# A pair's projection weights replaced while the last projection with the old ones runs, q and k rows in a ring of four at first, first weights in two parts

## The chip, the core and the metric

The kernel runs on one core of one Trainium2 chip. The metric is the device time of one execution in microseconds (us). Five engines work beside each other and meet only at semaphores: TensorE (PE, and PEld for its weight loads), VectorE (DVE), ScalarE (ACT), GpSimd (POOL) and SyncE (SP), which here only issues transfers.

## The reference, cut to what matters

One decoder layer is computed for 1024 prompt tokens and 64 sample tokens (8 sequences of 8) that share the weights.

```python
h = _rms_norm(x, attn_norm_g)
z = h @ w_in                                  # 1024 -> 3*512 (q, k, v) + 2*512 (a, g)
q = _rms_norm(q.reshape(N, T, 8, 64), q_norm_g)
k = _rms_norm(k.reshape(N, T, 8, 64), k_norm_g)
attn, k_state, v_state = attend(q, k, v)      # three dilated windows, combined
u = a * jax.nn.sigmoid(g)
c = _causal_depthwise(u_ext, conv_w, conv_b)  # 31 taps
c = jax.nn.silu(_layer_norm(c, conv_ln_g, conv_ln_b))
x = x + jnp.concatenate([attn, c], -1) @ w_out
h = _rms_norm(x, ffn_norm_g)
x = x + (jax.nn.silu(h @ w_gate) * (h @ w_up)) @ w_down
```

## The kernel before

Every large product is made of three matmuls (`mm3`): the weights and the activations are cut into a high part (fp32r) and a low part (the rest), and high times high, high times low and low times high are summed in PSUM. A piece of weights (128 x 1024, 512 KB) therefore goes three ways: SP loads it into a `raw` buffer, `high(n)` on ScalarE copies the high part, `low(n)` on VectorE (on GpSimd for some) subtracts to get the low part. `w_hi` and `w_lo` count the pieces.

The program is written out by hand, engine by engine, and its order on each engine is the order of the code. The stages:

- **Start.** x arrives in eight slices of 128 features. ScalarE cuts a slice (`xh`) and squares it (`xq`), VectorE subtracts (`xl`) and adds the squares up in `rb`. TensorE runs the first a/gate group over the slices k = 0 to 7, 18 matmuls for each, with the weights of the pieces 0 and 1. Before the last slice it sums the squares with a column of ones.
- **Conv inputs.** The groups g = 3 to 11 of a and gate, 48 matmuls each. From here on VectorE runs the 31 x 4 convolution taps (`tap`, two instructions each, 1024 prompt and 64 sample columns), spread by the tables `TAPS_AG`, `TAPS_Z0`, `TAPS_END0` and `TAPS_STEP` over whatever else it does.
- **First projection.** For the first pair of heads nine q/k/v projections z = 0 to 8 (one token tile each, 24 matmuls: `qkv(z)`). ScalarE squares q and k (`zsq`) and copies them to `zst`, a ring of two; VectorE sums the squares; ScalarE and VectorE make the root and its reciprocal; GpSimd multiplies the rows (`qk_norm`), TensorE turns them (`turn(z)`, issued ahead of `qkv(z + 2)`), GpSimd multiplies k by its gain and SP stores k from the same rows. The copy of z waits for the store of z - 2 (`k_st`).
- **Attention.** 40 steps n, ten for each of the four pairs of heads: step s = n mod 10 is a sample half (s = 0, 5) or one of eight prompt blocks. On TensorE a step is `scores(n + 1)`, the projection of one tile of the next pair (`qkv`, in steps s = 1 to 9; the last pair has pieces of the output projection and of the layer norm there, `fill`), `turn_probs(n)`, `values(n - 1)`, `turn`. On VectorE it is `mask_min(n + 1)` (mask and minimum of the scores), two or three taps, `normalise(n + 1)`, `square_sum` of the new tile. ScalarE takes the exponentials (`exps`) and copies the turned probabilities to `pt`. TensorE's `scores(n + 1)` waits for `mask_min(n)`, `turn_probs(n)` for `normalise(n)`.
- **Weights of the next pair.** A pair's three pieces lie in `wq`, 24 KB a partition, and are replaced when the last projection with the old ones is done: two high parts at the end of step s = 9 and one in step s = 0, the low parts on VectorE behind `mask_min` in the steps s = 0 (two) and s = 1 (one), where the first projection of the new tiles (s = 1) waits for them. The last pair's steps replace them by the first three pieces of the output projection.
- **Sample outputs.** The outputs of a sample half are scaled on VectorE (`scale_sample`, steps s = 2 and 7), turned on TensorE (`turn_sample`) and copied out of bank 6 on VectorE (`sample_outputs`); `values` of the next four blocks writes the same bank and waits for that copy (`d_se`).
- **After attention.** Output projection, second norm, and the feed-forward part in 11 chunks, from about 500 us to the end; neither is touched but for the place of one `low`.

Of the kernel before, what the change touches and what calls it, by code (L numbers as in the profile page):

```python
# [12 lines left out]
P = 128  # L13
# [92 lines left out]

def z_at(p, s):

    return NT * (p + 1) + s - 1 if p < NPAIR - 1 and s >= 1 else None
# [30 lines left out]
TAPS_STEP = {n: 2 if n % NSTEP in (0, 1, 6, 7) else 3 for n in range((NPAIR - 1) * NSTEP)}  # L140
# [3 lines left out]
def hymba_layer(nc, w_stream, xT, kT_c, v_c, cache_k, cache_v, stT, g1, g2, qg, kg, kgcol, cw, cb, lg, lb,  # L144
# [3 lines left out]
    with ExitStack() as ctx:  # L148
# [107 lines left out]
        def zbank(z):  # L256

            return bank(z % 4 if z < NT else 2 + z % 2, 384)
# [17 lines left out]
        raw_in = [sem(f"raw_in{i}") for i in range(3)]  # L276
        w_hi, w_lo = sem("w_hi"), sem("w_lo")
# [9 lines left out]
        k_st, v_st = [sem("k_stored0"), sem("k_stored1")], [sem(f"v_stored{p}") for p in range(NPAIR)]  # L287
        d_sk = [sem(f"sample_k_in{i}") for i in range(4)]
# [98 lines left out]
        def _(sp):  # L387
# [9 lines left out]
            piece(0)  # L397
            for k in range(4):
                sp.dma_start(xr[:, k, :], xT[k]).then_inc(x_in[k], 16)
                if k == 0:  # L400
                    piece(1)
            for k in range(4, KT):
                sp.wait_ge(x_lo, k - 3)
                sp.wait_ge(xsq, k - 3)
                sp.dma_start(xr[:, k % 4, :], xT[k]).then_inc(x_in[k], 16)
            for dst, src in ((ident[:], ident_d), (g2s, g2), (qgs, qg), (kgs[:], kg),
# [5 lines left out]
            for n in range(2, N_B + 3):  # L412
                piece(n)
# [10 lines left out]
            def store(z):  # L424
# [5 lines left out]
                k_src, v_src = zst[r, z % 2, P:2 * P], (vn[p % 2][:, t, :] if t < NT - 1 else vfar[r, 1, p % 2, :])  # L430
# [5 lines left out]
                sp.dma_start(k_dst, k_src).then_inc(k_st[z % 2], 16)  # L436
# [62 lines left out]
            for j in range(2):  # L499
                sp.wait_ge(k_st[j], 16 * NZ // 2)  # L500
# [13 lines left out]
        def _(pool):  # L514
# [25 lines left out]
            def qk_norm(z):  # L540

                r = ssz
                rows = zst[:, z % 2, :].rearrange("p (h d) -> p h d", d=DH)
                if z >= NT:
                    pool.wait_ge(z_ms, z - NT + 1)
# [5 lines left out]
            def k_gain(z):  # L551

                k_rows = zst[:, z % 2, P:2 * P]
# [75 lines left out]
        def _(pe):  # L629
# [9 lines left out]

            pe.wait_ge(t_zero, 1)  # L640
            pe.wait_ge(w_lo, 2)
            for k in range(KT):
                if k == KT - 1:
                    pe.wait_ge(mem_s, 1)
# [28 lines left out]
            def qkv(z):  # L673
# [6 lines left out]
                for k in range(KT):  # L680
                    if idx == 0:
# [3 lines left out]
                               k == 0, k == KT - 1)  # L685
                last.then_inc(z_mm, 1)

            def turn(z):
# [3 lines left out]
                for j in range(2):  # L692
                    cols = slice(j * P, (j + 1) * P)
                    if ZT[z % NT] < NT - 1:
                        pe.transpose(turned(j), zst[:, z % 2, cols], ident[:]).then_inc(z_tr, 1)
                    else:
                        pe.transpose(turned(j, NS), zst[P - NS:P, z % 2, cols],
# [1025 lines left out]
```

## Time and profile before

| | before |
|---|---|
| device time, median of 3 runs | 1361.35 us (1360.97 to 1363.18) |
| device time of the profiled execution | 1359.73 us |
| its span, first to last instruction | 1357.9 us |
| TensorE busy | 1312.9 us (97%), 9138 matmuls |
| VectorE busy | 660.7 us (49%) |
| ScalarE busy | 317.0 us (23%) |
| GpSimd busy | 416.1 us (31%) |
| mean granted TensorE clock | 0.989 |

The device time of the profiled execution is 1.8 us above its span, and 1.6 us under the median of the three timed runs. VectorE's share is an average over two halves: in the first 500 us it is busy for most of the time, behind that for about a third. A waiting engine other than TensorE costs nothing by itself; what counts is what TensorE waits for.

### The profile page before, as it was taken

The page shows a single profiled execution, that of the slowest core. Times are in us where ns is not written, and L with a number is a line of the kernel's source. Part 1 is how long each engine was busy: PE and PEld are TensorE (multiplying, and loading weights), DVE is VectorE, ACT ScalarE, POOL GpSimd, SP SyncE. Part 2 cuts the span into 40 slices and gives each one's busy share as a digit, 9 for nine tenths or more (in the row PEclk, how much of TensorE's full clock was granted, in tenths as well). Part 3 has the DMA queues.
Part 4 walks back from the last instruction along what each step waited for, and adds up shares of the span by engine and source line. Part 5 has one row for each costly group of instructions (what it writes and reads, how often), then busy time and mean ns, then how long its engine had stood idle before and what let it go on. Part 6 is the DMA issues. An engine that isn't in the chain of part 4 may idle for free.

```text
span 1357.9 us, 22625 instructions
## 1 busy us (share of the span) xinstructions
PE 1312.9 (97%) x9138; PEld 1253.9 (92%) x9138; DVE 660.7 (49%) x1247; ACT 317.0 (23%) x715; POOL 416.1 (31%) x278
## 2 busy tenths in 40 slices
PE   6999899898999999999999999999999999999998
PEld 6999778787877889999999999999999999999998
DVE  6598897987975665832313222231314141413134
ACT  6212444454454253421000000101010101010000
POOL 0231422232320025327343342523324243342220
PEclk9999999999998999999999999999999999999999
DMA  7224053334327120385114110231115111411103
GB/s 233 67 52 152 28 162 110 119 110 133 123 86 267 33 64 30 124 294 201 49 41 167 44 62 32 103 115 32 62 32 174 44 34 61 156 56 38 40 1 132
DMA packets 50694, 131.07 MB, mean 97 GB/s; under 512 B 14481, under 2 KB 26641, under 8 KB 50065
## 3 DMA queue, kind: packets, MB, share of 16 engines
q1 hardware_dynamic: 45088, 95.47, 21.4%
q10 hardware_dynamic: 5504, 34.11, 7.3%
q8 instruction: 81, 1.33, 0.4%
q14 instruction: 21, 0.16, 0.0%
HBM read 120.09 MB, written 43.28 MB: 120 GB/s over the span
## 4 chain that ended last, share of the span: by engine, by line
PE 89%; DVE 6%; POOL 1%; ACT 1%; DMA 1%; issue 1%; SPq 0%; ACTq 0%; DVEq 0%; POOLq 0%
PE ps L342 27%; PE ps L344 26%; PE ps L343 26%; PE ps L748 1%; PE ps L783 1%; PE ps L717 1%; DVE uc L1229 1%; PE ps L767 1%; DVE ml_c L1497 1%; PE ps L790 1%; PE ps L713 1%; POOL zst L549 1%; DVE wq L1339 1%; DMA out_nk_p<-zst 1%; PE ps L727 1%; PE ps L833 1%
## 5 line engine op out<-in xcount | busy, mean ns | idle before, releaser
L621 POOL TENSOR_TENSOR wf<-raw,small 128x1024 fp32r<-128x1024 f32 x60 | 113.9, 1898 | 432.6 <-PE ps L344 423.1
L1575 DVE TENSOR_TENSOR pr<-ps,sg 128x362 f32<-128x362 f32 (+1 forms) x66 | 35.3, 535 | 411.0 <-ACT sg L1189 411.0
L342 PE MATMUL ps<-mh_a,wf 128*128 128x362 f32 (+1 forms) x624 | 208.8, 335 | 6.2 <-DVE wf L1339 2.7
L343 PE MATMUL ps<-ml_a,wf 128*128 128x362 f32 (+1 forms) x624 | 205.9, 330 | 0.0
L344 PE MATMUL ps<-mh_a,wf 128*128 128x362 f32 (+1 forms) x624 | 205.8, 330 | 0.0
L344 PE MATMUL ps<-mh_c,wf 128*128 128x362 f32 (+1 forms) x624 | 204.5, 328 | 0.0
L343 PE MATMUL ps<-ml_c,wf 128*128 128x362 f32 (+1 forms) x624 | 204.5, 328 | 0.0
L342 PE MATMUL ps<-mh_c,wf 128*128 128x362 f32 (+1 forms) x624 | 204.0, 327 | 0.0
L1593 DVE TENSOR_TENSOR y<-ps,y 128x362 f32<-128x362 f32 (+1 forms) x264 | 139.2, 533 | 108.0 <-PE ps L344 108.0
L1229 DVE SCALAR_TENSOR_TENSOR uc<-uc,small 128x1024 f32<-128x1024 f32 x240 | 189.9, 853 | 0.3
L1189 ACT ACTIVATE sg<-ps 128x362 f32<-128x362 f32 (+1 forms) x66 | 31.3, 474 | 620.0 <-PE ps L344 620.0
L344 PE MATMUL ps<-ah,wf 128*128 128x364 f32 (+1 forms) x528 | 174.0, 330 | 0.0
L343 PE MATMUL ps<-al,wf 128*128 128x364 f32 (+1 forms) x528 | 173.7, 329 | 0.0
L342 PE MATMUL ps<-ah,wf 128*128 128x364 f32 (+1 forms) x528 | 173.4, 328 | 0.0
L623 POOL TENSOR_TENSOR wf<-raw,wf 128x1024 fp32r<-128x1024 f32 x60 | 147.4, 2457 | 4.7
L342 PEld LDWEIGHTS ps<-mh_a,wf 128*128 128x128 f32 x624 | 118.4, 190 | 11.3 <-issue 5.0
L344 PEld LDWEIGHTS ps<-mh_a,wf 128*128 128x128 f32 x624 | 118.6, 190 | 0.0
L343 PEld LDWEIGHTS ps<-ml_a,wf 128*128 128x128 f32 x624 | 118.2, 189 | 0.2
L342 PEld LDWEIGHTS ps<-mh_c,wf 128*128 128x128 f32 x624 | 117.8, 189 | 0.0
L343 PEld LDWEIGHTS ps<-ml_c,wf 128*128 128x128 f32 x624 | 117.7, 189 | 0.0
L344 PEld LDWEIGHTS ps<-mh_c,wf 128*128 128x128 f32 x624 | 117.6, 189 | 0.0
L342 PE MATMUL ps<-wq,xh 128*128 128x384 f32 x288 | 101.5, 352 | 10.4 <-DVE wq L1339 9.3
(149 smaller groups left out, 2076.4 us busy)
## 6 DMA issues: line engine op xcount, KB each, us to landing
raw<-in_w_stream SPq DMA_DIRECT2D x94, 512.0 KB, 3.5
skt<-in_kT_c SPq DMA_DIRECT2D x32, 384.0 KB, 4.7
sv<-in_v_c SPq DMA_DIRECT2D x32, 384.0 KB, 5.1
xr<-in_xT SPq DMA_DIRECT2D x8, 544.0 KB, 4.8
out_yT<-y SPq DMA_DIRECT2D x8, 544.0 KB, 2.7
y<-in_xT SPq DMA_DIRECT2D x1, 3264.0 KB, 17.3
out_nv_p<-vn SPq DMA_DIRECT2D x32, 64.0 KB, 2.0
out_nk_p<-zst SPq DMA_DIRECT2D x32, 64.0 KB, 1.6
```

The source lines that it names most:

```text
L342: e.matmul(out, wh, mh_, start=first, stop=False)
L343: e.matmul(out, wh, ml_, start=False, stop=False)
L344: return e.matmul(out, wl, mh_, start=False, stop=last)
L549: pool.tensor_tensor(rows, rows, r.unsqueeze(2).broadcast_to([P, 4, DH]), ALU.mult).then_inc(z_n, 1)
L621: pool.tensor_tensor(hi(m), src, zeros, ALU.add).then_inc(w_hi, 1)
L623: pool.tensor_tensor(lo(m), src, hi(m).bitcast(F32), ALU.subtract).then_inc(w_lo, 1)
L713: pe.matmul(ps[32 * r:32 * r + 32, h * 512:h * 512 + nf], q_[hr[h], i * P + 32 * r:i * P + 32 * r + 32], keys[:, r, :], start=True, stop=True)
L717: last = pe.matmul(bank(h, (i + 1) * P - k0, nf), q_[hr[h], i * P:(i + 1) * P], k_[hr[h], k0:(i + 1) * P], start=True, stop=True)
L1189: act.activation(sg[:, k6 % 2, 0:bn], bank(2 * (k6 % 2), bn), ACT.Silu).then_inc(gu_si, 1)
L1229: dve.scalar_tensor_tensor(out=dst, in0=src, scalar=w, in1=dst, op0=ALU.mult, op1=ALU.add).then_inc(s, 1)
L1575: dve.tensor_tensor(pr[:, k6 % 2, 0:bn], bank(2 * (k6 % 2) + 1, bn), sg[:, k6 % 2, 0:bn], ALU.mult).then_inc(gu_pr, 1)
L1593: dve.tensor_tensor(y[:, oc, b0:b0 + bn], bank(4 + m % 4, bn), y[:, oc, b0:b0 + bn], ALU.add).then_inc(dn_y, 1)
```

## The change

- **First weights in two parts.** Of the pieces 0 and 1 the first 128 columns (what slice k = 0 needs) are issued by ScalarE's own queue, and cut first; the other 896 columns follow x's first slice on SP. ScalarE's squares of a slice come one slice later. 18 matmuls on `ones_c` stand ahead of everything on TensorE. The pieces 2 and 3 are loaded and cut earlier.
- **Ring of four.** The q and k rows of z = 0 to 6 go to four places in `pt[:, 1]`, which nothing else uses yet; from z = 7 on `zst` is used as before. The projections' banks move from 0..3 to 2..5, so that `scores(0)` can stand ahead of `qkv(8)`. The tiles 7 and 8 get their root from GpSimd's power instead of ScalarE's root and VectorE's reciprocal.
- **Weights replaced during the last projection.** `w_free` counts when `qkv` of a pair's last tile has passed the first and the second third of `wq`; ScalarE's `next_weights` cuts the high parts then, and VectorE's low parts move into step s = 9 (two of them) and the start of step s = 0 (one).
- **Order around it.** `turn_sample` goes behind the step's projection or fill, `sample_outputs` behind the step's taps; one tap moves from step s = 9 to step s = 0; `low(E0 + 7)` goes ahead of the last `block_outputs`.

```diff
+ZP = 7
...
-TAPS_STEP = {n: 2 if n % NSTEP in (0, 1, 6, 7) else 3 for n in range((NPAIR - 1) * NSTEP)}
+TAPS_STEP = {n: 2 if n % NSTEP in (1, 6, 7, 9) else 3 for n in range((NPAIR - 1) * NSTEP)}
...
-            return bank(z % 4 if z < NT else 2 + z % 2, 384)
+            return bank(2 + (z % 4 if z < NT else z % 2), 384)
+
+        def zrows(z):
+            return pt[:, 1, (z % 4) * 2 * P:(z % 4 + 1) * 2 * P] if z < ZP else zst[:, z % 2, :]
...
             sp.dma_start(g1s, g1).then_inc(g_in, 16)
-            piece(0)
             for k in range(4):
                 sp.dma_start(xr[:, k, :], xT[k]).then_inc(x_in[k], 16)
                 if k == 0:
-                    piece(1)
+                    for n in range(2):
+                        sp.dma_start(raw[:, n, P:PC], w_stream[n, :, P:PC]).then_inc(raw_in[n], 16)
...
+            pe.wait_ge(mem_s, 1)
+            for _ in range(18):
+                pe.matmul(bank(7, P), ones_c[:], ones_c[:], start=True, stop=True)
             pe.wait_ge(t_zero, 1)
-            pe.wait_ge(w_lo, 2)
+            pe.wait_ge(k0_lo, 2)
             for k in range(KT):
+                if k == 1:
+                    pe.wait_ge(w_lo, 2)
...
+                    if idx == NT - 1 and k in (2, 5):
+                        last.then_inc(w_free, 1)
...
                 qkv(z)
+                if z == NT - 2:
+                    scores(0)
             turn(NT - 2)
-            pe.wait_ge(z_ev, NT)
-            scores(0)
...
                 if n + 1 < NALL:
                     scores(n + 1)
-                if s in (2, 7):
-                    turn_sample(p, s // 5)
                 if z_at(p, s) is not None:
                     qkv(z_at(p, s))
                 if fills:
                     fill(s, 0)
+                if s in (2, 7):
+                    turn_sample(p, s // 5)
+                if n == 0:
+                    pe.wait_ge(z_ev, NT - 1)
                 turn_probs(n)
...
+            for n in range(2):
+                act.dma_start(raw[:, n, 0:P], w_stream[n, :, 0:P]).then_inc(k0_in[n], 16)
+            act.wait_ge(zero_s, 1)
+            act.activation(small[:, 209:210], zero_c, ACT.Copy)
+            for n in range(2):
+                act.wait_ge(k0_in[n], 16)
+                act.activation(cut_to(n)[0][:, 0:P], raw[:, n, 0:P], ACT.Copy).then_inc(k0_hi, 1)
...
-                if z >= 2:
+                if 4 <= z < ZP:
+                    act.wait_ge(z_tr, 2 * (z - 3))
+                    act.wait_ge(k_sp[z % 4], 16)
+                if z >= ZP + 2:
                     act.wait_ge(z_tr, 2 * (z - 1))
-                    act.wait_ge(k_st[z % 2], 16 * (z // 2))
-                act.activation(zst[:, z % 2, :], src[:, 0:2 * P], ACT.Copy, scale=rs).then_inc(z_cp, 1)
-                if z < NT:
+                    act.wait_ge(k_st[z % 2], 16 * ((z - ZP) // 2))
+                act.activation(zrows(z), src[:, 0:2 * P], ACT.Copy, scale=rs).then_inc(z_cp, 1)
+                if z < ZP:
...
+            def next_weights(w0, j):
+                if j < 2:
+                    act.wait_ge(w_free, 2 * ((w0 - N_B) // 3 - 1) + j + 1)
+                high(w0 + j)
...
+                if s == NSTEP - 1 and p < NPAIR - 2:
+                    next_weights(w0, 0)
+                    next_weights(w0, 1)
                 if z_at(p, s) is not None:
                     keep(z_at(p, s))
+                if s == NSTEP - 1 and p < NPAIR - 2:
+                    next_weights(w0, 2)
...
             for z in range(NT):
+                if z == NT - 1:
+                    mask_min(0)
+                    low(N_B + 3)
+                    low(N_B + 4)
                 square_sum(z)
...
+                if s == 0 and 1 <= p < NPAIR - 1:
+                    low(N_B + 3 * (p + 1) + 2)
                 if n + 1 < NALL:
                     mask_min(n + 1)
-                if s in (2, 7):
-                    sample_outputs(p, s // 5)
...
-                if s == 0:
-                    low(w0)
-                    low(w0 + 1)
-                if s == 1:
-                    low(w0 + 2)
...
                 for _ in range(TAPS_STEP.get(n, 0)):
                     tap(done)
                     done += 1
+                if s in (2, 7):
+                    sample_outputs(p, s // 5)
...
                     normalise(n + 1)
+                if s == NSTEP - 1 and p < NPAIR - 2:
+                    low(N_B + 3 * (p + 2))
+                    low(N_B + 3 * (p + 2) + 1)
```

VectorE between the first projection and step n = 1, before. The two `wq` rows are the low parts of the second pair's first two pieces, `uc` rows are taps, ISA rows with `mks` or `mkp` are `mask_min`; the rows begin behind the last reciprocal of the projection.

```order
L1229 SCALAR_TENSOR_TENSOR uc<-uc,small 128x1024 [waits conv_prompt]
L1229 SCALAR_TENSOR_TENSOR uc<-uc,small 128x8x8 [waits conv_samples]
L1317 ISA tb,small<-ps,mks 128x800 [waits scores]
L1317 ISA small 128x1
L1326 RECIPROCAL small<-small 128x1 [waits exped]
L1317 ISA tb,small<-ps,mkp 128x128 [waits scores]
L1317 ISA small 128x1
L1339 TENSOR_TENSOR wq<-raw,wq 128x1024 [waits w_lo,w_hi]
L1339 TENSOR_TENSOR wq<-raw,wq 128x1024 [waits w_hi]
```

The same engine in the change, from the taps of z = 7 on (L1365 is `square_sum` of z = 8).

```order
L1291 SCALAR_TENSOR_TENSOR uc<-uc,small 128x8x8 [waits conv_samples]
L1390 ISA tb,small<-ps,mks 128x800 [waits scores]
L1390 ISA small 128x1
L1412 TENSOR_TENSOR wq<-raw,wq 128x1024 [waits w_lo,w_hi]
L1412 TENSOR_TENSOR wq<-raw,wq 128x1024 [waits w_hi]
L1365 TENSOR_REDUCE small<-zsq 128x4 [waits qkv_normed,qkv_squares]
L1368 TENSOR_SCALAR small<-small 128x4 [waits qkv_square_sums]
L1291 SCALAR_TENSOR_TENSOR uc<-uc,small 128x1024 [waits conv_prompt]
```

The mask of step 0 and two low parts have moved ahead of the last tile's sum of squares, its taps, and (further down) the mask of step 1.

VectorE at the end of step n = 9 and in step n = 10, before: the step's last tap, the reciprocal, the sum of squares of z = 17, `mask_min(11)`, then the two low parts.

```order
L1326 RECIPROCAL small<-small 128x1 [waits exped]
L1292 TENSOR_REDUCE small<-zsq 128x4 [waits qkv_normed,qkv_squares]
L1295 TENSOR_SCALAR small<-small 128x4 [waits qkv_square_sums]
L1317 ISA tb,small<-ps,mkp 128x128 [waits probs_turned,scores]
L1317 ISA small 128x1
...
L1339 TENSOR_TENSOR wq<-raw,wq 128x1024 [waits w_hi] x2
L1229 SCALAR_TENSOR_TENSOR uc<-uc,small 128x1024 [waits conv_prompt]
```

The same place in the change.

```order
L1399 RECIPROCAL small<-small 128x1 [waits exped]
L1412 TENSOR_TENSOR wq<-raw,wq 128x1024 [waits w_hi] x2
L1365 TENSOR_REDUCE small<-zsq 128x4 [waits qkv_normed,qkv_squares]
L1368 TENSOR_SCALAR small<-small 128x4 [waits qkv_square_sums]
L1412 TENSOR_TENSOR wq<-raw,wq 128x1024 [waits w_hi]
L1390 ISA tb,small<-ps,mkp 128x128 [waits probs_turned,scores]
```

All three low parts stand ahead of `mask_min(11)`; in the steps n = 11 and 12 the taps keep their places.

VectorE in step n = 2 (the same in every step s = 2), the change: `mask_min(3)`, three taps, then the copies of `sample_outputs` (`ao`), which before stood between the mask and the taps.

```order
L1390 ISA tb,small<-ps,mkp 128x288 [waits probs_turned,scores]
...
L1291 SCALAR_TENSOR_TENSOR uc<-uc,small 128x1024 [waits conv_prompt]
L1291 SCALAR_TENSOR_TENSOR uc<-uc,small 128x8x8 [waits conv_samples]
L1425 COPY ao<-ps 64x32 [waits sample_turned]
L1425 COPY ao<-ps 64x32
L1399 RECIPROCAL small<-small 128x2 [waits exped]
```

The copies now come behind six tap instructions; TensorE's `values(1)` waits for them.

## Rows read from the trace of the kernel before

**Rows 1.** The page's head: the span of the profiled execution.

```profile
span 1357.9 us, 22625 instructions
```

**Rows 2.** Waits of TensorE: line, releaser, us in total, times, longest.

```profile
PE ps L342 <- DVE ws L1238: 12.0, 1, 12.0
PE ps L342 <- DVE wq L1339: 9.3, 3, 3.6
PE ps L797 <- DVE so L1381: 4.2, 2, 2.8
...
PE ps L727 <- ACT vn L1033: 2.6, 1, 2.6
```

**Rows 3.** Windows: stretch, length, busy us of five engines, clock, DMA, GB/s.

```profile
12.00:17.60 5.60, 5.58 (x19) 5.60 (x20) 5.60 (x5) 5.60 (x6) 0.00 (x0) 1.00 0.66 201
17.60:35.50 17.90, 17.90 (x109) 17.90 (x109) 11.57 (x10) 9.07 (x9) 0.00 (x0) 1.00 0.71 185
165.00:181.00 16.00, 11.89 (x79) 8.46 (x83) 14.84 (x28) 9.37 (x23) 2.70 (x3) 0.80 0.45 134
181.34:184.67 3.33, 3.33 (x68) 2.52 (x61) 2.70 (x14) 1.56 (x7) 1.64 (x2) 1.00 0.35 95
322.00:335.00 13.00, 9.40 (x82) 7.91 (x83) 12.27 (x24) 6.38 (x17) 0.96 (x2) 0.88 0.53 167
```

**Rows 4.** The chain that ended last, 0 to 13 us: start, us, what.

```profile
1.20 3.99 DMA raw<-in_w_stream
```

**Rows 5.** Timeline of the first stage: start, us, engine, line, what.

```profile
7.52 1.19 ACT L969 ACTIVATE xh<-xr,small 128x1088 fp32r<-128x1088 f32 x1
8.79 1.35 DVE L1240 SCALAR_TENSOR_TENSOR xl<-xr,small,xh 128x1088 fp32r<-128x1088 f32 x1
...
35.57 2.06 PE L647 MATMUL ps<-ones_c,rb 128*128 128x1 f32 x18
...
40.57 1.03 PE L663 MATMUL ps<-ident,small 128*128 128x128 f32 x8
```

**Rows 6.** Timeline of ScalarE in the first projection: z = 0, 1, 7.

```profile
123.87 0.48 ACT L1020 ACTIVATE zsq<-ps,small 128x256 f32<-128x256 f32 x1 [4.43 <-PE ps L344]
...
128.03 0.47 ACT L1020 ACTIVATE zsq<-ps,small 128x256 f32<-128x256 f32 x1 [1.32 <-PE ps L344]
...
157.45 0.47 ACT L1020 ACTIVATE zsq<-ps,small 128x256 f32<-128x256 f32 x1 [1.15 <-PE ps L344]
```

**Rows 7.** Timelines of VectorE, ScalarE and GpSimd: single operations.

```profile
184.67 4.27 DVE L1229 SCALAR_TENSOR_TENSOR uc<-uc,small 128x1024 f32<-128x1024 f32 x6
...
237.63 0.99 DVE L1317 CUSTOM_DVE_ANT_0 tb<-ps,mks 128x800 f32<-128x800 f32 x1 [1.34 <-PE ps L727]
...
169.25 0.96 ACT L1066 ACTIVATE tb<-tb,small 128x800 f32<-128x800 f32 x1 [1.47 <-DVE small L1317]
...
170.21 1.04 ACT L962 ACTIVATE wq<-raw 128x1024 fp32r<-128x1024 f32 x1
...
160.26 1.81 DVE L1229 SCALAR_TENSOR_TENSOR uc<-uc,small 128x1024 f32<-128x1024 f32 x2
...
160.42 1.56 POOL L549 TENSOR_TENSOR zst<-zst,small 128x256 f32<-128x256 f32 x1 [2.63 <-DVE small L1435]
```

**Rows 8.** The chain that ended last: low parts of the pairs 2 and 3.

```profile
246.43 2.36 DVE wq L1339 x2
...
322.85 2.36 DVE wq L1339 x2
```

**Rows 9.** Timeline of TensorE: `values` of the steps 1, 11, 21, 31.

```profile
188.23 0.44 PE L783 MATMUL ps<-pt,vn 128*64 128x128 f32 x4
...
264.67 0.44 PE L783 MATMUL ps<-pt,vn 128*64 128x128 f32 x4
...
342.64 0.44 PE L783 MATMUL ps<-pt,vn 128*64 128x128 f32 x4
...
418.99 0.44 PE L783 MATMUL ps<-pt,vn 128*64 128x128 f32 x4
```

More of the change, by code:

```diff
@@ L104 @@
 NZ = NT * NPAIR
+ZP = 7
+K_ST = [16 * len([z for z in range(ZP, NZ) if z % 2 == j]) for j in range(2)]
+K_P = [16 * len([z for z in range(ZP) if z % 4 == j]) for j in range(4)]
 def z_at(p, s):
@@ L287, in hymba_layer @@
         k_st, v_st = [sem("k_stored0"), sem("k_stored1")], [sem(f"v_stored{p}") for p in range(NPAIR)]
+        k_sp = [sem(f"first_k_stored{j}") for j in range(4)]
+        w_free = sem("weights_free")
         d_sk = [sem(f"sample_k_in{i}") for i in range(4)]
@@ L405, in _ @@
                 sp.dma_start(xr[:, k % 4, :], xT[k]).then_inc(x_in[k], 16)
+            for n in range(2, 4):
+                piece(n)
             for dst, src in ((ident[:], ident_d), (g2s, g2), (qgs, qg), (kgs[:], kg),
@@ L411, in _ @@
                 sp.dma_start(ustate(c + 1, 0, PADC), stT[c]).then_inc(st_in, 16)
-            for n in range(2, N_B + 3):
+            for n in range(4, N_B + 3):
                 piece(n)
@@ L499, in _ @@
             for j in range(2):
-                sp.wait_ge(k_st[j], 16 * NZ // 2)
+                sp.wait_ge(k_st[j], K_ST[j])
+            for j in range(4):
+                sp.wait_ge(k_sp[j], K_P[j])
             for p in range(NPAIR):
@@ L1071, in copy_probs @@
                 act.wait_ge(d_pv, max(n - 1, 0))
+                if n == 1:
+                    for j in range(4):
+                        act.wait_ge(k_sp[j], K_P[j])
                 ends = (4 * P, 3 * P) if kind == "s" else (len(chunks(i)) * P,) * 2
@@ L1112, in _ @@
                     evict(turn_at(p, s), 1)
-                if s == NSTEP - 1 and p < NPAIR - 1:
-                    high(w0 + 3)
-                    high(w0 + 4)
+                if s == NSTEP - 1 and p == NPAIR - 2:
+                    high(E0 + 1)
+                    high(E0 + 2)
                 if p == NPAIR - 1:
@@ L1233, in _, with first_low, add_x_square @@
             done = 0
+            def first_low(n, cols, ready, done_s):
+                h, l = cut_to(n)
+                dve.wait_ge(ready, n + 1)
+                dve.tensor_tensor(l[:, cols], raw[:, n, cols], h[:, cols].bitcast(F32), ALU.subtract).then_inc(done_s, 1)
+            def add_x_square(k):
+                dve.wait_ge(xsq, k + 1)
+                if k >= 2:
+                    dve.wait_ge(x_ac, k - 1)
+                dve.tensor_tensor(rb[:], rb[:], xq[:, k % 2, :], ALU.add).then_inc(x_ac, 1)
+            for n in range(2):
+                first_low(n, slice(0, P), k0_hi, k0_lo)
             for k in range(KT):
[L1235 to L1238 removed]
                 dve.wait_ge(x_hi, k + 1)
@@ L1441, in _ @@
                     fill_qb(0)
+            low(N_B + 5)
             for _ in range(TAPS_END0):
@@ L1505, in _ @@
             rest(0, 1)
+            low(E0 + 7)
             block_outputs(2 * NPAIR - 1)
```

89 lines of the change are left out of this document (49 added, 40 removed).

## The prediction

> **What bounds the kernel now.** I read the page first: TensorE is busy for nearly the whole span of 1357.9 us [rows 1], so only its pauses and its slow stretches can give time back. The view of waits names the pauses: 12.0 us before the first matmul, three waits of 9.3 us together for the low parts of the next pair's weights, two of 4.2 us together for the scaled sample outputs, 2.6 us before the first scores [rows 2]. The windows show what TensorE does around them. From 12.0 to 17.6 us it starts 19 matmuls, 0.295 us each, from 17.6 to 35.5 us 109, 0.164 us each [rows 3]: the same work at the low level (1.2 GHz) and at the high one (2.4 GHz), although the clock column reads 1.00 in both, so at the start the spacing tells the level. From 165 to 181 us and from 322 to 335 us, both around a change of weights, the granted clock is 0.80 and 0.88 [rows 3]. In the first of these VectorE is busy for 14.84 of 16 us: there it is the bound, and TensorE waits for it. So each part below asks what VectorE still has in front of the thing that TensorE needs.
>
> **Start.** Before, the first piece of weights lands at 1.20 + 3.99 = 5.2 us [rows 4], then come a cut of the whole piece, x's slice and the second piece. Now x's first slice takes that place in the queue. It is 544 KB beside 128 KB of first columns, against 512 KB; I put its landing at 5.6 us (bounds 5.2, as the piece landed, and 5.2 × 672/512 = 6.8). The first columns are 64 KB each and are cut meanwhile. From the start of `xh` to the end of `xl` it is 10.14 − 7.52 = 2.6 us [rows 5], so the first matmul starts at 8.2 us instead of 12.0. Step k = 1 needs the other 896 columns cut twice on VectorE (7/8 of 1.18 us each, from two cuts in 2.36 us [rows 8]) and then its own `xl` of 1.35 us: 8.1 + 2.1 + 1.35 = 11.6, with a little for x's second slice 12.0 us. If the 18 matmuls on ones have brought TensorE to the high level, step 0 fits in before that, and six steps of 18 × 0.164 = 2.95 us follow: the sum of squares starts at 29.8 instead of 35.57 us [rows 5], 5.7 us earlier. The sum itself and step 7 (to 40.57) stay. VectorE's last sum of squares is ready by my count at 28.8 us, 1 us ahead. The price of the 18 matmuls isn't in the trace: at least 18 starts at the 2.06/18 us of the one-column matmuls [rows 5], 2.0 us; at most 18 × 4 × 0.295 × 128/364 = 7.5 us, four times the fp32r price at the low level. From 1.1 us that ends at 8.6 us at the latest, beside the wait for data; I take nothing. If the clock stays low, step 0 takes 5.4 us and the gain is 12.0 − 8.2 = 3.8. **Term: 5.7, bounds 3.8 and 6.1.** The early loads of the pieces 2 and 3 end a short wait behind this stage, but the evacuation of the first banks ends at almost the same moment; taken as nothing.
>
> **Ring of four.** The squares of z = 0 start at 123.87, of z = 1 at 128.03, of z = 7 at 157.45 us [rows 6]. One projection without turns is 4.16 us; with two transposes I put it at 4.36. Seven need 4.16 + 6 × 4.36 = 30.3 us, and took 33.6: 3.3 us go where the copy into the ring of two waits for the store and the turn comes late. What stays is the chain from a projection's end through squares, sum, root, reciprocal and GpSimd's multiply to the turn, which is about as long as a projection; I leave 0.1 us for each. **Term: 2.5, bounds 1.2 and 3.3.**
>
> **First change of weights.** Here the price moves rather than goes. TensorE may do `scores(0)` at once (2.6 us of wait less), but everything that it needs next comes from VectorE, which now has in one row, from the end of z = 7's squares (157.85) to the copies of `sample_outputs(0)`: 13 taps (2 + 2 + 1 + 3 + 2 + 3) at 4.27/3 = 1.42 us [rows 7], 18.5; three low parts at 1.18, 3.5; the sample mask 0.99; and the small work of two steps, 5.4 (one step had 2.70 us in a window without a tap [rows 3]). In front of the first low part it waits for the exponentials and a high part, 0.96 + 1.04 and their hand-overs, 2.2 us [rows 7]. Sum 30.6: the copies end at 188.5 us, and `values(1)`, which waits for them, stood at 188.23 [rows 9]. Before, the copies were done four taps earlier. TensorE's own work in this stretch is shorter and waits. **Term: −0.3, bounds −2 and +1.5.**
>
> **Second and third change.** VectorE is free for `mask_min(10)` at 237.63 [rows 7]. Up to the copies of step 12 it has that mask (0.99), ten taps (14.2), three low parts (3.5) and some 6.3 of small work (two steps and a block's copy, an estimate from the 2.70). It ends at 262.6; TensorE, without the wait of 3.6 us, is at `values(11)` at about 260.5 and waits 2.1. Before it was there at 264.67 [rows 9], so 2.1 us are left of the 3.6. In the third pair the same values stand at 342.64, 77.97 later, while the low parts lie 76.42 apart [rows 8, 9]: 1.5 us more were lost to the clock of 0.88. If the clock holds, that comes too. **Term: 2.1 + 3.6 = 5.7, bounds 1.0 and 9.0** (nothing but a shorter wait; or all of 3.6 + 3.6 + 1.5).
>
> **Last pair.** `turn_sample` now stands behind a `fill`, so its two waits, 2.8 and 1.4 us [rows 2], are filled with matmuls due anyway. `sample_outputs` stands behind one more cut of 1088 columns (about 1.3 us, as `xl` [rows 5]), so `values(31)`, now at 418.99 [rows 9], waits again: I put it at 416.3. **Term: 2.7 + 1.4 = 4.1, bounds 1.5 and 4.6.** The steps s = 7 have two taps and enough time; `low(E0 + 7)` moves within a row of VectorE work that is all due before the same matmul. Both nothing; if the cover in s = 7 fails, `values` waits under 1 us each time.
>
> **Sum.** 5.7 + 2.5 − 0.3 + 5.7 + 4.1 = 17.7. The profiled execution had 1359.73 us around its span of 1357.9 and would have 1342.0; from the median of the runs, 1361.35, it is **1343.6 us**.
>
> **A rule weighed.** A tap beside one of GpSimd's multiplies took 1.81 instead of 1.42 us, while the multiply took 1.56 [rows 7]: it cost VectorE 0.4 us. The Trainium skill, "SBUF — State Buffer", section "SBUF: two separate sides", says that a VectorE operation with two SBUF inputs and a GpSimd operation that reads SBUF exclude each other for the whole instruction. By the rule the tap would have grown by most of 1.56; by this row the overlap is mostly free.
>
> **Rivals.**
> - *VectorE doesn't bind.* If the taps leave room (waits of ScalarE overlap, small work costs less than 2.70 a step), the second and third change give 8.7 and the first the rest of its low-clock time, up to 5: 5.7 + 2.5 + 5 + 8.7 + 4.1 = 26, **1335 us**. For it: VectorE has 1.3 us of idle time before `mask_min(10)` [rows 7]. Against it: the 14.84 of 16 us.
> - *Taps and multiplies take turns.* If each multiply of GpSimd in these chains holds a tap back by its 1.56 us (three in the first, two in each of the others), VectorE ends 4.5 and 3 us later: the first change loses 4.8, the two others give only the clock's 1.5. 5.7 + 2.5 − 4.8 + 1.5 + 4.1 = 9.0, **1352 us**. This is what the Trainium skill's rule above would do here; the rows show a quarter of it, so its chance is small but counts.
> - *The clock falls in the new pauses.* TensorE keeps some ten pauses of 1 to 5 us. In the stretch at 0.80 it was at the low level for 40% of 16 us, which cost 3.2 us [rows 3]. From six such falls on that the old program did not have, 17.7 is eaten up; at seven the kernel takes **1366 us**, slower. Against it: the same pause of 3.6 us in the second pair was not followed by the 1.5 us that the third lost [rows 8, 9].
> - *The start alone stays low.* The ones don't raise the clock: 1.9 us less, 1345.5, inside the forecast.
>
> **Chances and range.** The forecast with its bounds (1338 to 1349) 0.62, VectorE not binding 0.15, taps and multiplies taking turns 0.19, the clock 0.04. The measurement of this kernel can tell about 0.2%, 2.7 us, from no change. Only the clock's rival ends above that or within it: faster 0.95, same 0.02, slower 0.03. The range leaves out the clock, the upper part of the second rival and the lower part of the first: 1336 to 1352.
>
> **What would show it.** The first matmul near 8 us with spacing 0.16 at once, the sum of squares at 30 us: the start. Squares 4.4 us apart and no wait for the store of k: the ring. No wait of a projection for low parts anywhere; instead waits of `scores(2)` for the mask of step 1, and of `values` in steps s = 2 for the copies, 0.5 to 2 us each: the moved price. No wait for the scaled outputs in the last pair. I am wrong if the waits of `values` are missing (first rival), if taps there take over 2.5 us (second), or if the clock of the stretches behind the changes is below 0.8 (third).

## The result, and the profile after

| | before | after |
|---|---|---|
| device time, median of 19 runs each | 1361.15 us | 1353.81 us (1346.15 to 1360.98) |
| ratio, 95% interval | | 0.995 (0.9938 to 0.9961) |
| profiled execution: device time, clock | 1359.73 us, 0.989 | 1348.85 us, 0.988 |

The kernel is faster by 7.3 us in the median and by 10.9 us between the two profiled executions; the forecast was 17.7, to 1343.6 us, with a range from 1336 to 1352. The 19 executions of the changed kernel lie 15 us apart and follow the granted clock: 1346.15 us at 0.990, 1360.98 at 0.980. The profiled one is the second fastest of them.

The waits of TensorE in the changed kernel (line, releaser, us in total, times, longest), beside [rows 2]:

```profile
span 1347.1 us, 22710 instructions
...
PE ps L355 <- DVE ml_c L1578: 7.3, 1, 7.3
PE ps L719 <- POOL zst L566: 5.7, 1, 5.7
PE ps L807 <- DVE ao L1425: 5.3, 3, 2.1
...
PE ps L741 <- DVE small L1390: 2.9, 1, 2.9
...
PE ps L807 <- DVE ml_a L1433: 1.5, 1, 1.5
```

The waits for data at the start, for low parts of `wq` (9.3) and for the scaled outputs `so` (4.2) are gone. The copies `ao`, the mask (`small`) and the last pair's `ml_a` make TensorE wait as the prediction said, the mask longer than it said (2.9 instead of 0.5 to 2 us). The two longest waits stand in no term of it. At the place of the longest one TensorE waited 2.7 us before:

```profile
PE ps L342 <- DVE wf L1339: 2.7, 1, 2.7
```

The same places as in [rows 5, 6, 9], from timelines of the changed kernel (start, us, engine, line, what, idle time before): the first matmul, the sum of squares, the squares of z = 0 and 7, `values` of the steps 1, 11, 21, the last `values`, the start of the output projection.

```profile
8.76 0.41 PE L355 MATMUL ps<-xh,ws 128*128 128x364 f32 x1 [1.38 <-DVE xl L1312]
...
29.95 2.06 PE L669 MATMUL ps<-ones_c,rb 128*128 128x1 f32 x18
...
117.31 0.48 ACT L1063 ACTIVATE zsq<-ps,small 128x256 f32<-128x256 f32 x1 [4.43 <-PE ps L357]
...
148.32 0.47 ACT L1063 ACTIVATE zsq<-ps,small 128x256 f32<-128x256 f32 x1 [2.35 <-PE ps L357]
...
180.87 0.44 PE L807 MATMUL ps<-pt,vn 128*64 128x128 f32 x4 [1.02 <-DVE ao L1425]
...
255.72 0.44 PE L807 MATMUL ps<-pt,vn 128*64 128x128 f32 x4 [2.13 <-DVE ao L1425]
...
330.55 0.44 PE L807 MATMUL ps<-pt,vn 128*64 128x128 f32 x4 [2.13 <-DVE ao L1425]
...
471.29 0.66 PE L807 MATMUL ps<-pt,vn 128*64 128x128 f32 x8
...
486.42 0.65 PE L355 MATMUL ps<-mh_a,wf 128*128 128x364 f32 x1 [7.33 <-DVE ml_c L1578]
```

The last two stood at 487.62 and 498.12 us before. Read against each other, each stage has its gain:

| stage, up to | lead over before, us | gained in the stage | forecast |
|---|---|---|---|
| start, squares of z = 0 | 6.56 | 6.56 | 5.7 |
| ring, squares of z = 7 | 9.13 | 2.57 | 2.5 |
| first change, `values(1)` | 7.36 | -1.77 | -0.3 |
| second and third, `values(21)` | 12.09 | 4.73 | 5.7 |
| last pair, last `values` | 16.33 | 4.24 | 4.1 |
| start of the output projection | 11.70 | -4.63 | 0 |
| end | 10.8 | -0.9 | 0 |

Up to the end of attention the forecast holds within 1.4 us in this execution (16.33 against 17.7). Then 4.6 us go at one place. VectorE, then GpSimd, there:

```profile
478.42 0.55 DVE L1578 TENSOR_TENSOR ml_c<-uc,mh_c 128x384 fp32r<-128x384 f32 x1
...
479.34 2.14 DVE L1578 TENSOR_TENSOR ml_c<-uc,mh_c 128x384 fp32r<-128x384 f32 x1
...
482.29 1.82 DVE L1578 TENSOR_TENSOR ml_c<-uc,mh_c 128x384 fp32r<-128x384 f32 x1
...
484.03 2.24 DVE L1578 TENSOR_TENSOR ml_c<-uc,mh_c 128x384 fp32r<-128x384 f32 x1
```

```profile
479.17 1.89 POOL L553 TENSOR_TENSOR wf<-raw,small 128x1024 fp32r<-128x1024 f32 x1 [36.28 <-PE ps L357]
481.14 2.55 POOL L555 TENSOR_TENSOR wf<-raw,wf 128x1024 fp32r<-128x1024 f32 x1
483.65 2.21 POOL L553 TENSOR_TENSOR wf<-raw,small 128x1024 fp32r<-128x1024 f32 x1
```

The same place before: VectorE's second cut, then the third and fourth, and GpSimd's first.

```profile
494.53 0.55 DVE L1497 TENSOR_TENSOR ml_c<-uc,mh_c 128x384 fp32r<-128x384 f32 x1
...
495.91 1.02 DVE L1497 TENSOR_TENSOR ml_c<-uc,mh_c 128x384 fp32r<-128x384 f32 x2
...
498.19 2.09 POOL L536 TENSOR_TENSOR wf<-raw,small 128x1024 fp32r<-128x1024 f32 x1 [40.38 <-DVE wf L1339]
```

Four equal cuts (`cut_swish(0, c)`): in the changed kernel the first, alone, takes 0.55 us, the others 2.14, 1.82, 2.24. Each of these ends 0.4 us after one of GpSimd's operations has ended. The excess is 6.20 - 1.65 = 4.55 us, the 4.6 of the table. GpSimd's first cut waits for the last fillers of TensorE (`f_mm`) and for `w_lo` at F0, and `low(E0 + 7)` is the piece that completes this count. Before, the low part came last (the row names `wf L1339`). Moved ahead on VectorE, it is done at 476.4 us, TensorE's matmul comes last (`ps L357`), and GpSimd goes three cuts early. So these two engines meet not only at semaphores, as the introduction has it: VectorE's cuts end with operations of GpSimd to which no semaphore ties them. The Trainium skill, "SBUF — State Buffer", section "SBUF: two separate sides", says that of a VectorE operation with two SBUF inputs and a GpSimd operation that reads SBUF, whichever starts first has the shared ports for the whole instruction. These rows agree with it.

The stretch of the first change, GpSimd, then TensorE:

```profile
158.54 1.98 POOL L563 TENSOR_TENSOR small<-small 128x4 f32<-128x4 f32 x1 [5.62 <-DVE small L1368]
160.60 0.92 POOL L566 TENSOR_TENSOR zst<-zst,small 128x256 f32<-128x256 f32 x1
```

```profile
161.57 0.69 PE L719 MATMUL ps<-ident,zst 128*128 128x128 f32 x2 [5.70 <-POOL zst L566]
165.13 1.22 PE L741 MATMUL ps<-kt,qt 64*128 64x256 f32 x4 [2.88 <-DVE small L1390]
```

TensorE waits first for the last tile's chain (sum, power, multiply), then for the mask of step 1 at the end of VectorE's row.

### The profile page after: what moved, and what is told of

It reads as the page before. It is cut to its first block, busy times and chain, and to the rows that moved or that the text cites. A ratio compares the mean times of both kernels' runs of the same rounds, so it can differ in the third digit from the quotient of the medians.

```text
span 1347.1 us, 22710 instructions
## 1 busy us (share of the span) xinstructions
PE 1310.9 (97%) x9174; PEld 1254.5 (93%) x9174; DVE 662.5 (49%) x1249; ACT 317.6 (24%) x716; POOL 426.0 (32%) x280
## 4 chain that ended last, share of the span: by engine, by line
PE 89%; DVE 9%; issue 1%; ACT 0%; DMA 0%; POOL 0%; ACTq 0%; DVEq 0%; POOLq 0%
PE ps L355 27%; PE ps L357 27%; PE ps L356 27%; DVE uc L1291 3%; PE ps L772 1%; PE ps L741 1%; PE ps L807 1%; PE ps L737 1%; PE ps L814 1%; PE ps L751 1%; PE ps L791 1%; DVE wq L1412 1%; DVE tb L1390 1%; PE ps L719 1%; PE ps L857 1%
## 5 line engine op out<-in xcount | busy, mean ns | idle before, releaser
L357 PE MATMUL ps<-mh_a,wf 128*128 128x362 f32 (+1 forms) x624 | 205.8, 330 | 0.0
L357 PE MATMUL ps<-mh_c,wf 128*128 128x362 f32 (+1 forms) x624 | 204.7, 328 | 0.0
L357 PE MATMUL ps<-ah,wf 128*128 128x364 f32 (+1 forms) x528 | 174.0, 330 | 0.0
L357 PEld LDWEIGHTS ps<-mh_a,wf 128*128 128x128 f32 x624 | 118.6, 190 | 0.0
L357 PEld LDWEIGHTS ps<-mh_c,wf 128*128 128x128 f32 x624 | 117.7, 189 | 0.8 <-issue 0.6
```

The costliest lines, as they stand in the source:

```text
L357: return e.matmul(out, wl, mh_, start=False, stop=last)
```

## The experiments

### The low part of the output projection's last piece

`e1_low_back`: the changed kernel with the old order.

```diff
-            low(E0 + 7)
             block_outputs(2 * NPAIR - 1)
...
             cut_swish(0, 3)
+            low(E0 + 7)
```

> The changed kernel with the low part of the last piece of the output projection back in its old place, behind the four cuts of the first block. Theory A (GpSimd's cuts of the next weights are released 20 us earlier on their side and take turns with VectorE's cuts of the same moment): the three cuts beside them take 0.55 us again instead of 2.14, 1.82 and 2.24, the output projection waits about 2.7 us instead of 7.3 and starts 4.6 us earlier than the 486.4 us of the changed kernel; the median falls by 4.6 us, by more if the long pause also brings low-clock stretches in other executions. Theory B (the loss lies elsewhere, in low-clock stretches earlier in the program; the low part would be waited for as before): the projection starts within 1 us of 486.4 and the median stays at 1353.8, with the same spread of some 15 us.

`e2_low_early_alone`: the opposite edit, alone, in the kernel before.

> The kernel before with nothing but this low part moved ahead of the last block's outputs. Theory A: GpSimd's four cuts start some 20 us after the last filler as soon as the last sum is in, beside VectorE's cuts of the first block; the output projection starts 4 to 5 us later than the 498.1 us of before, the median rises to about 1366. Theory B: all VectorE work in that row is due before the same matmul, its order doesn't matter: 1361, the same.

`e3_gpsimd_held`: the new order stays, and GpSimd waits.

```diff
             pool.wait_ge(w_lo, F0)
+            pool.wait_ge(n_lo, sum(NP_LN[:1]))
             cut(F0)
```

> The changed kernel, the low part left early, but GpSimd's cuts of the feed-forward weights wait until VectorE has cut the first block. Theory A: what costs is that both engines work on SBUF at once, not the order on VectorE: the output projection starts near 481.8 us, 4.6 us earlier, as with the low part back in its place, median near 1349. Theory B (the order of VectorE's row itself costs): starts at 486 as in the changed kernel, or later, since the cuts of the feed-forward weights are late as well.

The start of the output projection in e1, e2 and e3, from their timelines of TensorE:

```profile
485.16 0.43 PE L355 MATMUL ps<-mh_a,wf 128*128 128x364 f32 x1 [2.70 <-DVE wf L1412]
```

```profile
504.21 0.64 PE L342 MATMUL ps<-mh_a,wf 128*128 128x364 f32 x1 [7.33 <-DVE ml_c L1497]
```

```profile
489.42 0.41 PE L355 MATMUL ps<-mh_a,wf 128*128 128x364 f32 x1 [2.78 <-DVE ml_c L1579]
```

The wait is 2.7 us wherever GpSimd starts late, 7.33 wherever it starts early, in both kernels. The absolute places differ with what the clock did before; from the last `values` to this matmul it is 10.50 us before, 15.13 after, 10.49 in e1, 15.12 in e2, 10.58 in e3. e3 has VectorE's new order and no loss, so the order on VectorE costs nothing, the meeting with GpSimd 4.6 us. The times: e2 1365.45 us against 1361.96, ratio 1.0027 (1.0014 to 1.004), about 3.7 us slower; e3 1350.67, ratio 0.9924 (0.9909 to 0.9938); e1 1352.10, 0.9939 (0.9922 to 0.9957), which overlaps with the changed kernel's interval (e3's touches it). Shown by the traces and by e2; the time of e1 alone wouldn't have shown it. Theory B fell in all three as far as the place goes, but the median fell by 1.7 us in e1 and by 3.1 in e3, not 4.6, and stayed 7 to 8.5 us above the forecast. Why it fell by less than 4.6 stays open.

### The matmuls on ones

`e4_no_ones`: the changed kernel without the 18 matmuls.

> The changed kernel without the 18 matmuls on ones ahead of the first group. Theory A (they bring TensorE to its high level before the data is there): the matmuls from 8.8 us on start 0.29 us apart instead of 0.165, step k = 1 starts at 14 us instead of 12.0, the sum of squares about 2 us later; median 1.9 to 2.5 us up. Theory B (the level rises without them): spacing 0.165 from 8.8 us on, median the same. A third outcome, that the spread between executions changes by much more than 2 us, would show that the start decides where the executions differ.

TensorE at the start of e4, one line of `mm3`:

```profile
8.43 0.64 PE L355 MATMUL ps<-xh,ws 128*128 128x364 f32 x1 [8.43 <-DVE xl L1310]
9.47 0.51 PE L355 MATMUL ps<-xh,ws 128*128 128x364 f32 x1
10.38 0.50 PE L355 MATMUL ps<-xh,ws 128*128 128x362 f32 x1
11.29 0.51 PE L355 MATMUL ps<-xh,ws 128*128 128x362 f32 x1
12.06 0.33 PE L355 MATMUL ps<-xh,ws 128*128 128x362 f32 x1
12.56 0.33 PE L355 MATMUL ps<-xh,ws 128*128 128x362 f32 x1
13.06 0.33 PE L355 MATMUL ps<-xh,ws 128*128 128x364 f32 x1
```

Groups of three lie 0.91 us apart at first, 0.50 from 12 us on: the low and the high level. Theory A in kind; the size is 1 us instead of 1.9, because the low level ends within step 0, so that step k = 1 starts at 13.06 instead of 12.03 us (11.64 to 12.16 in the eleven profiles with the ones). The sum of squares starts at 30.90 us instead of 29.95. Median 1355.09, 1.3 us above the changed kernel; the intervals overlap (0.9945 to 0.9975), so the time alone does not show it.

### The pauses before values

`e5_copies_first`: in the first three pairs `turn_sample` ahead of the projection and `sample_outputs` ahead of the taps again, GpSimd held.

> The changed kernel with GpSimd's cuts held (median 1350.7 us), and in the first three pairs the sample outputs turned ahead of the projection and copied ahead of the taps, as before the change. Theory A (the three waits of values of 5.3 us together are there only because the copies stand behind three taps, and each such pause also lets the clock fall in some executions): the waits are gone, values of the steps 1, 11 and 21 come 1, 3 and 5 us earlier, the stretches behind them keep the high clock; median near 1345, less spread. Theory B (VectorE binds in the whole stretch, so the wait goes to the next mask or the next turned probabilities): 0 to 1.5 us less, other waits of the same size.

`e6_tap_to_step6`, GpSimd held (in the table of taps, two instead of three in the steps s = 2):

```diff
-TAPS_STEP = {n: 2 if n % NSTEP in (1, 6, 7, 9) else 3 ...
+TAPS_STEP = {n: 2 if n % NSTEP in (1, 2, 7, 9) else 3 ...
```

> The changed kernel with GpSimd's cuts held, one tap of the steps s = 2 moved to the steps s = 6 in the first three pairs. Theory A (in the steps 0 to 2 VectorE's row decides when values can go, one tap is 1.4 us of it; step 6 has more than 1.5 us of idle time on VectorE): the three waits shrink from 5.3 to about 1.5 us, median 3 to 4 us below 1350.7. Theory B: the wait comes up again in step 6, or the low clock behind the pauses doesn't depend on their length: within 1.5 us of 1350.7.

`e11_tap_to_step2`: the same table with four taps in s = 2 and two in s = 3.

> The opposite dose: GpSimd's cuts held, one tap more in the steps s = 2 (four), one less in the steps s = 3. Theory A (each pause for the copies costs its length, and a low-clock stretch behind it in a part of the executions that is already large at 2.1 us): waits of values 5.3 + 4.3 = 9.6 us, median 4 to 5 us above 1350.7. Theory B (longer pauses bring more low clock): 6 us and more above. Theory C (VectorE isn't what values waits for): the same.

Waits for the copies in e6 and in e11:

```profile
PE ps L808 <- DVE ao L1426: 1.5, 2, 0.7
```

```profile
PE ps L808 <- DVE ao L1426: 9.0, 3, 3.5
```

| | waits for `ao` | median | ratio (95%) |
|---|---|---|---|
| e6, one tap less | 1.5 us | 1344.59 us | 0.9877 (0.9862 to 0.9892) |
| e3 | 5.3 us | 1350.67 us | 0.9924 (0.9909 to 0.9938) |
| e11, one tap more | 9.0 us | 1357.06 us | 0.9978 (0.9964 to 0.9991) |
| e5, copies first | none (2.6 for `so`) | 1344.04 us | 0.9868 (0.9852 to 0.9883) |

Theory A held for the median and the waits of e5 and, with a larger gain than it expected, of e6; theory B held for e11. From e3 on, 3.8 us of waits less give 6.1 us (6.4 by the ratios), 3.7 more cost 6.4 (7.3 by the ratios), and in e5 2.7 less give 6.6. By the medians a pause costs more than its length, 1.6 to 2.5 times; the waits are those of one execution each, so the factor is rough. Where the rest goes is seen in windows around `values(11)`: length, busy us of five engines, then the granted clock (third number from the end). The changed kernel:

```profile
252.00:260.00 8.00, 5.87 (x53) 4.87 (x52) 7.39 (x18) 3.36 (x11) 3.26 (x4) 1.00 0.35 131
```

The run e7 (below), with the same code and the same pause there:

```profile
252.00:260.00 8.00, 7.05 (x40) 5.82 (x41) 6.45 (x18) 1.72 (x6) 2.04 (x3) 0.57 0.27 82
```

The run e11, around `values(11)` and `values(21)`:

```profile
256.00:264.00 8.00, 5.53 (x39) 4.48 (x40) 7.03 (x18) 1.81 (x7) 3.12 (x3) 0.79 0.05 17
332.00:344.00 12.00, 8.48 (x54) 7.00 (x53) 9.83 (x24) 3.36 (x11) 2.03 (x3) 0.72 0.43 146
```

The run e6 at the same two places:

```profile
250.00:258.00 8.00, 7.27 (x63) 6.18 (x61) 7.40 (x18) 3.74 (x13) 3.02 (x3) 1.00 0.37 135
324.00:336.00 12.00, 11.27 (x103) 8.92 (x102) 10.71 (x27) 6.21 (x19) 5.29 (x6) 1.00 0.53 185
```

Behind a pause of 2.1 us the clock fell to the low level in one execution (0.57) and not in the other (1.00); behind 3.5 us it fell at both changes; behind 0.7 us at neither. The other profiles say what such a fall costs. The clock is that of the 8 us from each of the two `values` on:

| | pauses at `values(11)`, `values(21)` | clock behind them | from one to the other |
|---|---|---|---|
| changed kernel | 2.1, 2.1 us | 1.00, 1.00 | 74.83 us |
| e3 | 2.1, 2.1 us | 0.79, 0.79 | 76.38 us |
| e1, e4, e7 | 2.1, 2.1 us | 0.57, 0.79 | 77.72 to 77.75 us |
| e6, e9, e10, e12 | 0.7, 0.7 us | 1.00, 1.00 | 73.42 to 73.45 us |

With the same pauses at both ends, a fall costs 1.5 us in e3 and 2.9 in e1, e4 and e7. The profile of the changed kernel happens to be the one of these five without a fall there. Without the pauses for the copies the clock is not safe either: the profile of e5, the slowest of its four executions (1349.64 us), has 0.79 from 252 to 260 us, around a wait of 1.3 us for `so`.

### The weights themselves

`e8_old_2nd_3rd_change`: high and low parts of the second and third change at their old places, taps as before around them, GpSimd held.

> The changed kernel with GpSimd's cuts held, the second and third change of weights undone: high and low parts at their old places, taps as before around them. Theory A (the forecast's term, as the profile of the changed kernel has it at full clock): values of step 11 come 76.4 instead of 74.8 us behind those of step 1, of step 21 76.4 to 78.0 instead of 74.8 behind those of step 11; median 3.5 to 5 us up, at 1354 to 1356. Theory B (the new pause for the copies lets the clock fall about as often as the old one, so most is given back): 1 to 2 us up.

The waits for `wq` are back (7.2 us in two), those for the copies fall to 1.8. Values of step 11 come 77.2 us behind those of step 1, of step 21 78.5 behind those of step 11 (e3: 74.8 and 76.4), together 4.5 us later. Median 1353.56, 2.9 us above e3; ratio 0.9952 (0.9934 to 0.9971), by the ratios 3.8 us above. This lies between both theories or at the lower end of A: the term that I put at 5.7 is worth 4.7 in the one profile without falls and 2.9 to 3.8 over the executions.

`e7_first_row_short`: GpSimd held, three taps taken out of the row between the last tile's sum of squares and the mask of step 1.

```diff
+                if z == NT - 1:
+                    break
...
-            for _ in range(TAPS_END0):
-                tap(done)
-                done += 1
...
-TAPS_STEP = {n: 2 if ...
+TAPS_STEP = {n: 4 if n in (3, 4, 5) else 2 if ...
```

> The changed kernel with GpSimd's cuts held, the three taps between the last tile's sum of squares and the mask of step 1 moved to the steps 3, 4 and 5. Theory A (in the first change VectorE's row is what TensorE waits for): the mask of step 1 is done about 4.5 us earlier, the wait of 2.9 us for it disappears, that of values(1) too, values(1) comes 33 - 4 = 29 us behind the squares of z = 7 (32.55 before), median 3 to 4 us below 1350.7. Theory B (the chain of the last tile through GpSimd's power and multiply, the 5.7 us wait, is the bound): values(1) at 31.5 to 32.5 us behind these squares, and four taps in the steps 3 to 5 may cost something there: within 1.5 us of 1350.7.

The wait for the mask is gone and `values(1)` comes 30.1 us behind the squares of z = 7 (32.55 before the edit): 2.4 us, between the theories. What is left is the wait for the turned rows, 6.0 us: the chain of the last tile. The median, 1350.09, is 0.6 us below e3, by the ratios (0.9906, 0.989 to 0.9922) 2.4 us; the intervals overlap, so the times do not settle the gain.

### Put together

`e9_both_tap_moves`: the tables of e6 and e7, GpSimd held.

> GpSimd's cuts held, the tap moved from step 2 to step 6, and the three taps of the first change moved to the steps 3 to 5. Theory A (the two moves act at different places): the 2.4 us that the shorter first row gave in its profile come on top, without the pauses at the steps 11 and 21: median near 1342. Theory B (what the first row gives is lost to the clock behind its own pause of 5.7 us, as the median of that run, 1350.1 against 1350.7, suggests): 1344 to 1345.

Theory A: 1340.6 us, ratio 0.9859 (0.9841 to 0.9877), 4.0 us below e6 by the medians and 2.4 by the ratios, with overlapping intervals; `values(1)` 28.6 us behind the squares.

`e10_sum_first`: e9 with the last tile's sum of squares ahead of the low parts.

```diff
                 if z == NT - 1:
                     mask_min(0)
-                    low(N_B + 3)
-                    low(N_B + 4)
                 square_sum(z)
+                if z == NT - 1:
+                    low(N_B + 3)
+                    low(N_B + 4)
```

> The same with the last tile's sum of squares ahead of the two low parts on VectorE. Theory A (the wait of 5.7 to 6.0 us for the turned rows is the chain sum, power, multiply, and the low parts stand in front of the sum): the sum comes at about 156.9 instead of 157.5 to 157.9 us of a program whose squares of z = 7 lie at 148, the wait shrinks by 0.5 to 1 us, the power (2.0 us beside a low part) stays long since the low parts now run beside it. Theory B (the squares on ScalarE, behind two high parts, are what is late): no change of the wait.

TensorE in e10, at the turned rows and at the mask of step 1:

```profile
161.19 0.69 PE L720 MATMUL ps<-ident,zst 128*128 128x128 f32 x2 [4.42 <-POOL zst L566]
...
162.75 1.23 PE L742 MATMUL ps<-kt,qt 64*128 64x256 f32 x4 [0.87 <-DVE small L1391]
```

The wait shrinks by 1.6 us, more than expected, and 0.9 come back as a wait for the mask. In this profile nothing is gained: `values(1)` comes 29.4 us behind the squares of z = 7 (e9: 28.6), and from 14.5 to 21.5 us behind these squares the granted clock is 0.62 (e9: 0.81). Median 1339.49, ratio 0.9839 (0.9825 to 0.9853): its interval overlaps with e9's, so a gain is not shown.

`e12_held_longer`: e9 with GpSimd's cuts behind all sixteen cuts.

```diff
-            pool.wait_ge(n_lo, sum(NP_LN[:1]))
+            pool.wait_ge(n_lo, sum(NP_LN))
```

> As the run with both moves of taps, but GpSimd's cuts wait for all sixteen cuts of VectorE, so that none of them runs beside the other. Theory A (an operation of either engine with its data in SBUF waits for the other's to end, so VectorE's twelve cuts took 11.7 us beside GpSimd's and would take 5): the cuts shrink to 0.2 to 0.55 us each, the wait of 1.7 us for the first sums y is gone, 1 to 2 us less than the run beside it. Theory B (GpSimd's later weights are then what the first gate group waits for): 0 to 5 us more.

All sixteen cuts in e9, then in e12 (ns: shortest/median/longest):

```profile
L1578 DVE TENSOR_TENSOR ml_c<-uc,mh_c x16: 211/550/2426, 471.8 to 486.5; 128x384 fp32r<-128x384 f32 x8, 128x256 fp32r<-128x256 f32 x4, 128x64 fp32r<-128x64 f32 x4
```

```profile
L1578 DVE TENSOR_TENSOR ml_c<-uc,mh_c x16: 219/488/554, 473.3 to 482.8; 128x384 fp32r<-128x384 f32 x8, 128x256 fp32r<-128x256 f32 x4, 128x64 fp32r<-128x64 f32 x4
```

No cut takes longer than 0.55 us now, and the wait of 1.7 us for the sums `y` that e9 has is gone. From the start of the output projection to the end it is 858.3 us instead of 861.4. Median 1337.41, ratio 0.9836 (0.9821 to 0.985): the lowest median of this study, 23 us below before; its interval still overlaps with e9's. The weights that GpSimd cuts later were not missed: TensorE waits for none of them.

## Why the prediction was wrong

- **The step that failed** is the sentence that `low(E0 + 7)` "moves within a row of VectorE work that is all due before the same matmul". That is true of VectorE. But the piece's count is also what GpSimd waited for, and GpSimd then ran beside cuts that TensorE needs at once: 4.6 us where I had nothing (e1, e2, e3). Before, the same operations met behind the last of these cuts: the row x12 took 11.66 us, and TensorE waited 0.2 us for the sums `y` behind it.
- **The rule that I weighed** came out, and my row had been misread: I had left out that the first to start keeps its time. In [rows 7] the tap (160.26) starts before the multiply (160.42). The tap's large instruction keeps its time (1.25 us), and the multiply pays: 1.56 us, where the median of the 36 multiplies is 0.61. The tap's small instruction, which starts behind the multiply, pays the 0.4 us that I found. The price falls on the later one. I looked for it on the tap alone and concluded that the overlap was mostly free. Later in the changed kernel GpSimd's power takes 1.01 us beside VectorE work that reads PSUM, where it took 1.98 beside taps. The multiply behind it comes level with a tap and takes 0.61; there the six tap instructions pay, 4.68 us instead of 4.26. GpSimd, then VectorE:

```profile
174.66 1.01 POOL L563 TENSOR_TENSOR small<-small 128x4 f32<-128x4 f32 x1 [11.34 <-DVE small L1368]
175.75 0.61 POOL L566 TENSOR_TENSOR zst<-zst,small 128x256 f32<-128x256 f32 x1
```

```profile
165.00 4.26 DVE L1291 SCALAR_TENSOR_TENSOR uc<-uc,small 128x1024 f32<-128x1024 f32 x6
...
175.74 4.68 DVE L1291 SCALAR_TENSOR_TENSOR uc<-uc,small 128x1024 f32<-128x1024 f32 x6
```

- **Clock.** The rival of the clock falling in the new pauses had 0.04 and was priced as seven falls together. In fact the clock fell behind the pauses of 2.1 us in four of five profiles, at 1.5 to 2.9 us each. I priced the remaining waits of `values` at their length; they cost more than that. Without them and the meeting with GpSimd the kernel is at 1344.0 to 1344.6 us (e5, e6). That this is the forecast's 1343.6 is luck: the forecast had these pauses in it.
- **The other rivals.** The measured 1353.8 lies near the 1352 of taps and multiplies taking turns, but not by that mechanism: it had the first change at -4.8 and the two others at 1.5, measured are -1.77 and 4.73, and no tap instruction of the first change took over 1.70 us. The sign of the clock's rival was there, at the first change: 0.68 from 155 to 171 us.
- **Second and third change: 5.7.** The wait for the copies is 2.13 us as forecast (2.1). The gain at full clock is 4.73: 1.59 at the second change and 3.14 at the third, for 2.1 and 3.6. In e3, whose clock fell behind both pauses, it is 1.60 and 1.59 (74.84 and 76.38 us, against 76.44 and 77.97 before). The mechanism was right, the size too large, by what the clock takes back above all.
- **First change: -0.3.** Measured -1.77, inside the bounds. The miss lies in VectorE's row, which is busy from the first low part to the copies: they end at 180.72 us, 31.9 behind the end of the squares of z = 7 (forecast 30.6), and TensorE's `values(1)` waits 1.02 us for them. The 13 taps took 19.9 us instead of 18.5 and the three low parts 3.85 instead of 3.5, two taps taking 3.2 us beside GpSimd's power and multiply and 2.87 where GpSimd was idle. GpSimd's power and multiply I priced nowhere: TensorE waits 5.7 us for that chain, earlier. With VectorE's row shorter it is what TensorE waits for, so e7 gains 2.4 us from three taps. (The squares of z = 7 ended at 157.92 us before, not at 157.85; that changes nothing.)
- **Start, ring, last pair.** 6.56, 2.57 and 4.24 against 5.7, 2.5 and 4.1. The matmuls on ones took 6.3 us, within the bounds of 2.0 and 7.5. The first matmul came at 8.76 (8.2), step k = 1 at 12.03 (12.0), the sum of squares at 29.95 (29.8), 5.62 earlier than before; the other 0.94 us of the stage come behind it and stood in no term. That VectorE's last sum was ready in time was luck: in five of the eleven profiles with this start (e3, e5, e10, e11, e12) TensorE waits 0.75 to 0.87 us for it. In e5 GpSimd's low part of piece 2 starts first (27.09 us) and the addition (27.39) takes 3.29 us; in e6 the addition starts at 27.38, GpSimd at 27.39, and the addition takes 1.29.

The sum in the profiled execution: 17.7 - 4.6 (GpSimd) - 1.5 (first change) - 1.0 (second and third) + 0.9 + 0.1 + 0.1 (start, ring, last pair) - 0.9 (behind) = 10.8. From there to the 7.3 us of the medians the clock is what differs most: 0.988 in the profile, 0.985 on average over the executions, at 1.5 us for each thousandth 4.5 of the 5.0 us between the two. Which falls those executions had can't be seen without their traces, so this last part is argued, not shown.

## What to carry to other kernels

A moved instruction moves every count that it raises: list who waits for that count on the other engines, and what their work will then run beside. Where two engines slow each other, look for the price on the one that started second, not on the one that you care about. A pause of TensorE that you leave in place is priced above its length, and a table of small work (here the taps) can take it away at once: one tap in each step s = 2 moved gave 6.1 us (e6 against e3) where the whole change gave 7.3.

## What the hardware showed unexpectedly

- VectorE's cuts (both inputs in SBUF) and GpSimd's cuts do not share time but exclude each other: 0.55 us alone, 1.8 to 2.2 us behind an operation of GpSimd, which in turn took 3.88 us in e9 where VectorE's cuts had started first (1.89 in e12, alone).
- The same pause of 2.1 us, with the same code around it, kept the high clock behind it in one profile (1.00) and not in four others (0.57 or 0.79): 19 executions of the changed kernel lie 15 us apart, five of e12, with shorter pauses, 2.8 us.
- Which of two such operations pays can turn on a start a few tenths of a us earlier: VectorE's last addition of the squares took 1.29 us or 3.3, by whether it or GpSimd's low part came first.
